# Final norm and stores inside the last group of the second feed-forward stage

## The chip, the cores and the metric

The kernel runs on one core of a Trainium2 chip. The metric is the time of one execution on the device in microseconds (us). The core has TensorE (PE: matmuls, and transposes through the matmul path), VectorE (DVE), ScalarE (ACT), GpSimd (POOL) and SyncE (SP, whose queue issues the DMAs). PSUM has eight banks of 128x512 f32.

## The reference

One decoder layer for 1024 prompt tokens and 64 sample tokens (8 sequences of 8), width 1024: a half-step feed-forward, a mixing block (RWKV and windowed attention), a second half-step feed-forward, and a final RMS norm. What the change touches is the end:

```python
x = x + 0.5 * gt3 * swiglu(modulate(x, norm_ffn2, sh3, sc3), ffn2_w_gu, ffn2_w_down)
y = x * lax.rsqrt(jnp.mean(x * x, axis=-1, keepdims=True) + 1e-5) * norm_final
```

The rows of y are stored as `y_prompt` (1024 x 1024) and `y_sample` (64 x 1024), f32.

## The kernel before

x lies transposed in SBUF: `k.x` is [128, 8, 1088], channel 128*c + p on partition p, chunk c, all 1088 tokens along the free axis. `ffn` (L657) is used for both feed-forward stages. It works in `NGRP` = 11 groups of 256 hidden channels. A group first makes the gate and up products, six pairs into PSUM banks 0 to 3 (`up`), with Silu on ACT (`swish`) and the product on DVE (`gated`), and then 24 down products (`down`): three token tiles t of 364, 364 and 360 tokens, and for each the eight output chunks c, so product v = 8*t + c, six matmuls in fp32r each (three passes over two hidden chunks). Product v goes into bank 4 + v % 4. `summed` on DVE adds it, gated, into x (`add_gated`, L490); for the third token tile, which has 296 prompt tokens and the 64 sample tokens, this is three instructions (L490, L493, L495), with a drain between the last two. The semaphore `dn_mm` says that a product is done, `dn_free` that its bank is free. In the second stage PE runs groups 1 to 10 in one loop. In the first stage (`first`) the last group is written out and has work of the next norm among its down products: square and mean (L338, L347), a root (L355) and scaling (L381).

After the second stage its block ends, and `store_output` (L2840) makes the final norm in a block of its own. It takes nine tiles of 128 tokens (the last has the 64 sample tokens), with two sets of buffers. For a tile DVE copies x into `x_now` (L2868), PE turns it in eight transposes into two banks (L2899), ACT squares both banks with row sums (L2911), DVE adds the two sums (L2875), ACT takes the root (L2915), DVE inverts it (L2877) and multiplies the two banks by it and by the norm's weight into `y_rows` (L2883), and SP stores the rows (L2930, L2932). The weight, one row broadcast over 128 partitions, is loaded at the start of that block (L2923). On each engine the tiles go in order; the loop body has two tiles.

Of the kernel before, what the change touches and what calls it, by code (L numbers as in the profile page):

```python
# [28 lines left out]
P = 128  # L29
D = 1024  # L30
# [625 lines left out]

def ffn(k, name, w_gu, w_down, i_shift):  # L657
# [35 lines left out]
    else:  # L693
        gate, gate_turned, gate_n = Ada(k, "gate2", [WT_AT + KB * a for a in (24, 32, 40, 48)], 7), k.psum[7][:, 256:512], 0
    LATE = range(1, 4) if first else range(1, 1)

    with nc.Block() as block:  # L697
        @block.sync
        def _(sp):
# [50 lines left out]
            if first:  # L750
                sp.wait_ge(up_lo_done, FC * NGRP)
                win.load(sp, 0, win.first[0])
                win.load(sp, 1, win.first[1])
                for t, (a, n) in enumerate(TILES):
                    sp.wait_ge(x_final, 2 * t + 2)
                    sp.dma_start(k.dram["x_spill"][:, :, a:a + n], k.x[:, :, a:a + n]).then_inc(k.spilled, 16)

        @block.gpsimd
        def _(pool):
# [22 lines left out]
            if first:  # L782
                win.low(pool, 0)
                mix.odd_lows(pool, 0)

        @block.tensor
        def _(pe):
# [8 lines left out]
            def down(g, t, c):  # L796
# [4 lines left out]
                pe.wait_ge(dn_free, ND * g + v + 1)  # L801
                three_passes(pe, k.psum[4 + v % 4][:, 0:n],
# [47 lines left out]
            def last_group():  # L850
# [6 lines left out]
                pe.wait_ge(dn_lo_done, g + 1)  # L857
                for t in range(NT):
# [16 lines left out]
            with pe.Fori(LATE.stop, NGRP - (1 if first else 0)) as g:  # L875
                group(g)
            if first:
                last_group()

        @block.scalar  # L880
        def _(act):
# [19 lines left out]
            if first:  # L901
# [5 lines left out]
                mix.highs(act, 0, True)  # L907

        @block.vector
        def _(dve):  # L910
# [25 lines left out]
            def summed(g, v):  # L936
                t, c = v // KD, v % KD
                dve.wait_ge(dn_mm, ND * g + v + 1)
                add_gated(dve, k, i_gate, c, t, k.psum[4 + v % 4], scratch[:, v % 2]).then_inc(dn_free, 1)
# [31 lines left out]
            def last_group():  # L971
# [3 lines left out]
                if not first:  # L975
                    for v in range(ND):
                        summed(g, v)
# [1862 lines left out]
def store_output(k):  # L2840

    x_now = [k.at(f"x_now{j}", WT_AT + 4096 * j, [P, KD, P]) for j in range(2)]
    rows = [k.at(f"y_rows{j}", WT_AT + 4096 * (2 + j), [P, D]) for j in range(2)]
    squares = k.at("y_squares", WT_AT + 4096 * 4, [P, D])
    weight = k.at("y_weight", WT_AT + 4096 * 5, [P, D])
    sums = [k.at(f"y_sums{j}", WT_AT + 4096 * 6 + 32 * j, [P, 4]) for j in range(2)]
    weight_in, now_done, turned, sq_done, sum_done, root_done, rows_done = (
        k.sem(f"y_{n}") for n in ("weight_in", "now_done", "turned", "sq_done", "sum_done", "root_done", "rows_done"))
    y_out = [k.sem(f"y_out{j}") for j in range(2)]
    NTT = NP_TOK // P  # L2850
    yv = k.dram["y_prompt"][0].rearrange("(i j p) n -> j p i n", p=P, j=2)

    def tiles(eng, body):

        with eng.Fori(0, NTT // 2 - 1) as i:  # L2855
            for j in range(2):
                body(i, j, P, P)
        body(NTT // 2 - 1, 0, P, P)
        body(NTT // 2 - 1, 1, P, NS_TOK)
        body(NTT // 2, 0, NS_TOK, 0)  # L2860

    with k.nc.Block() as block:  # L2862
        @block.vector
        def _(dve):
            def take(i, j, n):

                dve.wait_ge(turned, 2 * i + j + 1)
                dve.tensor_scalar(x_now[j][:, :, 0:n], k.x[:, :, bass.ds(256 * i + 128 * j, n)], 1.0, None, ALU.mult  # L2868
                                  ).then_inc(now_done, 1)

            def tile(i, j, n, n_next):
                if n_next:
                    take(i + j, 1 - j, n_next)
                dve.wait_ge(sq_done, 2 * i + j + 1)
                dve.tensor_tensor(sums[j][0:n, 2:3], sums[j][0:n, 0:1], sums[j][0:n, 1:2], ALU.add).then_inc(sum_done, 1)  # L2875
                dve.wait_ge(root_done, 2 * i + j + 1)
                dve.reciprocal(sums[j][0:n, 3:4], sums[j][0:n, 3:4])  # L2877
                dve.drain()  # L2878

                dve.wait_ge(y_out[j], 16 * i + 16)  # L2880
                for h in range(2):
                    col = slice(512 * h, 512 * h + 512)
                    ins = dve.scalar_tensor_tensor(rows[j][0:n, col], k.psum[2 * j + h][0:n, :], sums[j][0:n, 3:4],  # L2883
                                                   weight[0:n, col], ALU.mult, ALU.mult)
                ins.then_inc(rows_done, 1)

            dve.sem_inc(rows_done, 2)
            take(0, 0, P)
            dve.wait_ge(weight_in, 16)
            tiles(dve, tile)  # L2890

        @block.tensor
        def _(pe):
            def tile(i, j, n, n_next):
                pe.wait_ge(now_done, 2 * i + j + 1)

                pe.wait_ge(rows_done, 2 * i + j + 1)
                for c in range(KD):
                    ins = pe.transpose(k.psum[2 * j + c // 4][0:n, P * (c % 4):P * (c % 4) + P], x_now[j][:, c, 0:n],  # L2899
                                       k.c("ident"))  # L2900
# [77 lines left out]
```

## Time and profile before

| | us |
|---|---|
| median of 3 runs | 2534.65 |
| lowest, highest | 2529.38, 2535.4 |
| profiled execution | 2534.88 |
| its span | 2532.9 |
| PE busy in the span | 2401.2 (95%) |
| DVE busy | 1117.5 (44%) |
| ACT busy | 387.7 (15%) |
| POOL busy | 526.4 (21%) |

The profile is of one execution. Times in its rows count from the start of the span. A busy PE is not PE at its peak. PEclk is the clock granted to PE as a share of full speed: 1.00 is 2.4 GHz, 0.50 is 1.2 GHz. What an idle time is put down to is inferred from semaphores.

### The profile page before, as it was taken

What the parts mean: (1) busy time and instruction counts of PE and PEld (TensorE: products, weight loads), DVE (VectorE), ACT (ScalarE), POOL (GpSimd) and SP (SyncE); (2) the same over time, 40 slices, a digit from 0 to 9 for tenths busy, and PEclk for the clock granted to TensorE, in tenths of its full rate; (3) what the DMA queues carried; (4) which work ended last, traced back from release to release, by engine and by line L of the source; (5) the groups of instructions that cost most, each with busy time, mean ns of one, the idle gap of its engine ahead of it and who ended that gap; (6) DMA issues with size and microseconds to landing.
All of it is one profiled execution on the core that took longest, in us unless ns stands there. A gap on an engine that the chain in (4) does not pass through costs nothing. (4 is left out here: it accounts for less than half of the span.)

```text
span 2532.9 us, 51980 instructions
## 1 busy us (share of the span) xinstructions
PE 2401.2 (95%) x22210; PEld 2277.4 (90%) x22210; DVE 1117.5 (44%) x2477; ACT 387.7 (15%) x879; POOL 526.4 (21%) x270
## 2 busy tenths in 40 slices
PE   5999999999999899999788889989999999999996
PEld 4999999999999899888377775979999999999995
DVE  4533434333344454343666663137333444443336
ACT  4100000000000223344611132031000000000003
POOL 3312122121121131111511034123211212212200
PEclk8999999999999999999799997989999999999997
DMA  9223221111111221011310012122111111111102
GB/s 328 84 100 100 69 80 50 50 50 33 50 28 38 87 79 55 26 34 39 117 25 5 5 32 86 42 100 84 51 33 50 28 38 50 50 50 50 33 0 79
DMA packets 160616, 151.19 MB, mean 60 GB/s; under 512 B 21472, under 2 KB 141969, under 8 KB 160072
## 3 DMA queue, kind: packets, MB, share of 16 engines
q1 hardware_dynamic: 159944, 146.75, 18.3%
q8 instruction: 117, 1.92, 0.3%
q10 hardware_dynamic: 144, 2.23, 0.2%
q14 instruction: 27, 0.22, 0.0%
q0 software_dynamic: 384, 0.07, 0.0%
HBM read 137.98 MB, written 11.34 MB: 59 GB/s over the span
## 5 line engine op out<-in xcount | busy, mean ns | idle before, releaser
L475 PE MATMUL bank<-hh,f_up_hi 128*128 128x364 f32 (+1 forms) x2112 | 697.1, 330 | 9.4 <-ACT hh L415 9.4
L477 PE MATMUL bank<-hh,f_up_lo 128*128 128x364 f32 (+1 forms) x2112 | 695.1, 329 | 0.0
L476 PE MATMUL bank<-hl,f_up_hi 128*128 128x364 f32 (+1 forms) x2112 | 695.0, 329 | 0.0
L928 DVE TENSOR_TENSOR f_prod<-f_silu,bank 128x364 f32<-128x364 f32 x132 | 70.2, 532 | 779.7 <-PE bank L477 779.7
L475 PEld LDWEIGHTS bank<-hh,f_up_hi 128*128 128x128 f32 x2112 | 398.1, 188 | 15.8 <-issue 15.4
L490 DVE SCALAR_TENSOR_TENSOR x<-bank,mods,x 128x364 f32<-128x364 f32 (+2 forms) x552 | 310.4, 572 | 201.4 <-PE bank L477 184.4
L476 PEld LDWEIGHTS bank<-hl,f_up_hi 128*128 128x128 f32 x2112 | 398.2, 189 | 0.0
L477 PEld LDWEIGHTS bank<-hh,f_up_lo 128*128 128x128 f32 x2112 | 398.0, 188 | 0.0
L762 POOL TENSOR_TENSOR f_up_lo<-f_up_raw,f_up_hi 128x2048 fp32r<-128x2048 f32 x44 | 202.9, 4612 | 818.4 <-DVE f_up_hi L915 818.4
L475 PE MATMUL bank<-f_a_hi,f_dn_hi 128*128 128x364 f32 (+1 forms) x1056 | 347.4, 329 | 0.0
L477 PE MATMUL bank<-f_a_hi,f_dn_lo 128*128 128x364 f32 (+1 forms) x1056 | 346.9, 328 | 0.0
L476 PE MATMUL bank<-f_a_lo,f_dn_hi 128*128 128x364 f32 (+1 forms) x1056 | 346.9, 328 | 0.0
L887 ACT ACTIVATE f_silu<-bank 128x364 f32<-128x364 f32 x132 | 62.5, 474 | 1458.3 <-PE bank L477 1458.3
L475 PEld LDWEIGHTS bank<-f_a_hi,f_dn_hi 128*128 128x128 f32 x1056 | 198.5, 188 | 0.3
L476 PEld LDWEIGHTS bank<-f_a_lo,f_dn_hi 128*128 128x128 f32 x1056 | 198.5, 188 | 0.0
L477 PEld LDWEIGHTS bank<-f_a_hi,f_dn_lo 128*128 128x128 f32 x1056 | 198.5, 188 | 0.0
L767 POOL TENSOR_TENSOR f_dn_lo<-f_dn_raw,f_dn_hi 128x2048 fp32r<-128x2048 f32 x22 | 102.3, 4649 | 389.7 <-DVE f_dn_hi L921 389.7
L475 PE MATMUL bank<-hh,w_in_hi 128*128 128x364 f32 (+1 forms) x480 | 164.3, 342 | 9.1 <-PEq L697 8.2
L476 PE MATMUL bank<-hl,w_in_hi 128*128 128x364 f32 (+1 forms) x480 | 159.6, 333 | 0.0
L477 PE MATMUL bank<-hh,w_in_lo 128*128 128x364 f32 (+1 forms) x480 | 159.5, 332 | 0.0
L475 PEld LDWEIGHTS bank<-hh,w_in_hi 128*128 128x128 f32 x480 | 92.1, 192 | 22.2 <-issue 21.7
L1052 POOL TENSOR_TENSOR w_in_lo<-w_in_raw,w_in_hi 128x1024 fp32r<-128x1024 f32 x18 | 47.0, 2612 | 224.7 <-DVE w_in_hi L1047 224.7
(380 smaller groups left out, 2854.4 us busy)
## 6 DMA issues: line engine op xcount, KB each, us to landing
f_up_raw<-in_ffn_w_gu SPq DMA_DIRECT2D x88, 512.0 KB, 5.0
f_dn_raw<-in_ffn_w_down SPq DMA_DIRECT2D x22, 1024.0 KB, 7.6
ada<-in_w_ada SPq DMA_DIRECT2D x12, 1024.0 KB, 16.1
late<-in_w_ada SPq DMA_DIRECT2D x12, 1024.0 KB, 4.8
w_in_raw<-in_w_in SPq DMA_DIRECT2D x16, 512.0 KB
gates<-in_w_ada SPq DMA_DIRECT2D x8, 1024.0 KB, 7.0
x_in<-in_x_prompt SPq DMA_DIRECT2D x8, 512.0 KB, 8.8
gate<-in_w_ada SPq DMA_DIRECT2D x4, 1024.0 KB, 11.2
```

The source lines that it names most:

```text
L475: pe.matmul(out, wh, rh, start=(n == 0), stop=False)
L476: pe.matmul(out, wh, rl, start=False, stop=False)
L477: ins = pe.matmul(out, wl, rh, start=False, stop=(n == last))
L490: ins = dve.scalar_tensor_tensor(x[:, a:a + np_], bank[:, 0:np_], gate[:, 0:1], x[:, a:a + np_], ALU.mult, ALU.add)
L762: pool.tensor_tensor(up_lo[j][:], up_raw[:], up_hi[j][:].bitcast(F32), ALU.subtract).then_inc(up_lo_done, 1)
L767: pool.tensor_tensor(dn_lo[:], dn_raw[:], dn_hi[:].bitcast(F32), ALU.subtract).then_inc(dn_lo_done, 1)
L887: act.activation(silu[u % 2][:, 0:n], k.psum[2 * (u % 2)][:, 0:n], ACT.Silu).then_inc(gate_free, 1)
L928: dve.tensor_tensor(prod[u % 2][:, 0:n], silu[u % 2][:, 0:n], k.psum[2 * (u % 2) + 1][:, 0:n], ALU.mult).then_inc(up_free, 1)
L1052: pool.tensor_tensor(lo[:], self.raw_of(n)[:], hi[:].bitcast(F32), ALU.subtract).then_inc(self.lo_done, 1)
```

## The change

`store_output` goes. A class `Outputs` gives the same work to the block of the second feed-forward stage, where the last group is now written out.

- The nine tiles have 128, 128 and 108 tokens in each of the first two token tiles, and 128, 128 and 104 in the third (40 prompt and 64 sample tokens), so each lies in one token tile. They are turned straight from `k.x`, with no copy.
- A tile takes two banks: 0 and 1, 2 and 3, or 6 and 7. The down products of the third token tile use banks 4 and 5 alone. Each tile has its own row buffer (`y_rows0` to `y_rows8`), in the room of the weights that are used up.
- ACT takes an Identity of one sum (scaled, plus eps), then the Sqrt of the other with that as bias, in place of DVE's addition.
- Tiles 0 to 5 are handled whole between the products; of tiles 6 to 8 the first four chunks are turned after products 21 to 23 and squared, and DVE multiplies that half by the weight alone. After the last product chunks 4 to 6 and then 7 are turned, ACT squares the second half, DVE scales it, and POOL scales the first half by the inverse.
- The weight's load is issued when the last up weights have been split. Each tile has its store; the last has two.

```diff
+class Outputs:
+    TOKENS = [(0, 128), (128, 128), (256, 108), (364, 128), (492, 128), (620, 108), (728, 128), (856, 128), (984, 104)]
+    SETS = [0, 1, 0, 1, 0, 2, 1, 0, 2]
+    LAST = 6
...
+    def pe_tile(self, pe, j):
+        pe.wait_ge(self.x_final, j // 3 + 1)
+        if 2 <= j <= 4:
+            pe.wait_ge(self.rows_done, j - 1)
+        self.turn(pe, j, range(KD)).then_inc(self.turned, 1)
+
+    def pe_first_half(self, pe, j):
+        pe.wait_ge(self.x_final, 2 + 4)
+        pe.wait_ge(self.rows_done, j - 2)
+        self.turn(pe, j, range(4)).then_inc(self.turned, 1)
+
+    def pe_end(self, pe):
+        pe.wait_ge(self.x_final, 2 + KD - 1)
+        for j in range(self.LAST, len(self.TOKENS)):
+            self.turn(pe, j, range(4, KD - 1))
+        pe.wait_ge(self.x_final, 2 + KD)
+        for j in range(self.LAST, len(self.TOKENS)):
+            self.turn(pe, j, range(KD - 1, KD)).then_inc(self.turned, 1)
...
+    def root(self, act, j):
+        act.drain()
+        act.activation(self.col(j, 2), self.col(j, 1), ACT.Identity, scale=1.0 / D, bias=self.k.c("eps")[0:self.TOKENS[j][1]])
+        act.drain()
+        act.activation(self.col(j, 3), self.col(j, 0), ACT.Sqrt, scale=1.0 / D, bias=self.col(j, 2)).then_inc(self.root_done, 1)
+
+    def act(self, act):
+        for j in range(self.LAST):
+            act.wait_ge(self.turned, j + 1)
+            self.square(act, j, 0)
+            self.square(act, j, 1)
+            self.root(act, j)
+        for j in range(self.LAST, len(self.TOKENS)):
+            act.wait_ge(self.turned, j + 1)
+            act.drain()
+            self.square(act, j, 0).then_inc(self.squared, 1)
+        for j in range(self.LAST, len(self.TOKENS)):
+            act.wait_ge(self.turned, j + 4)
+            self.square(act, j, 1)
+            self.root(act, j)
...
+    def scaled(self, dve, j):
+        self.inverse(dve, j)
+        if j == 0:
+            dve.wait_ge(self.weight_in, 16)
+        for h in ((0, 1) if j < self.LAST else (1,)):
+            ins = dve.scalar_tensor_tensor(self.row(j, h), self.bank(j, h), self.col(j, 3),
+                                           self.weight[0:self.TOKENS[j][1], D // 2 * h:D // 2 * h + D // 2], ALU.mult, ALU.mult)
+        ins.then_inc(self.rows_done, 1)
...
 @@ sync
+            else:
+                sp.wait_ge(up_lo_done, FC * NGRP)
+                sp.dma_start(outputs.weight[:], k.dram["norm_final"].rearrange("(o n) -> o n", o=1).broadcast_to([P, D])
+                             ).then_inc(outputs.weight_in, 16)
+                outputs.sync(sp)
 @@ tensor, last group
+                    for c in range(KD):
+                        down(g, 0, c)
+                    pe.wait_ge(gate_free, NU * NGRP + 2)
+                    pe.wait_ge(up_free, NU * NGRP + 2)
+                    for c in range(KD):
+                        down(g, 1, c)
+                        if c in (1, 3, 5):
+                            outputs.pe_tile(pe, c // 2)
+                    for c in range(KD):
+                        down(g, 2, c, 2)
+                        if c in (0, 1, 2):
+                            outputs.pe_tile(pe, 3 + c)
+                        if c in (5, 6, 7):
+                            outputs.pe_first_half(pe, c + 1)
+                    outputs.pe_end(pe)
 @@ vector, last group
-                        summed(g, v)
+                        t, c = v // KD, v % KD
+                        summed(g, v, 2 if t == 2 else 4)
+                        if c == KD - 1 or t == 2:
+                            dve.drain().then_inc(outputs.x_final, 1)
+                        if t == 1 and c in (4, 6):
+                            outputs.scaled(dve, c // 2 - 2)
+                        if t == 2 and c in (0, 2, 3, 5):
+                            outputs.scaled(dve, (2, None, 3, 4, None, 5)[c])
+                        if t == 2 and c >= 6:
+                            outputs.weighted(dve, c)
+                    outputs.weighted(dve, 8)
+                    for j in range(outputs.LAST, len(outputs.TOKENS)):
+                        outputs.scaled(dve, j)
 @@ build
-        store_output(k)
```

## Rows read from the trace of the kernel before

**Rows 1.** Windows: busy us of PE, PEld, DVE, ACT, POOL; PEclk, DMA share, GB/s.

```profile
2480.00:2490.00 10.00, 10.00 (x62) 10.00 (x61) 6.86 (x17) 0.00 (x0) 0.00 (x0) 1.00 0.00 0
2500.00:2534.00 34.00, 15.69 (x64) 12.22 (x64) 19.23 (x44) 17.91 (x45) 0.00 (x0) 0.50 0.34 131
```

**Rows 2.** Timeline, last products and sums: start, duration, what, idle before.

```profile
2482.97 0.60 DVE L490 SCALAR_TENSOR_TENSOR x<-bank,mods,x 128x364 f32<-128x364 f32 x1 [0.41 <-PE bank L477]
...
2493.58 0.33 PE L477 MATMUL bank<-f_a_hi,f_dn_lo 128*128 128x360 f32 x1
...
2493.95 0.53 DVE L490 SCALAR_TENSOR_TENSOR x<-bank,mods,x 128x296 f32<-128x296 f32 x1
...
2494.70 0.23 DVE L495 TENSOR_TENSOR x<-x,f_scratch 128x64 f32<-128x64 f32 x1
```

**Rows 3.** Timeline of PE, transposes of the first two tiles.

```profile
2496.10 1.10 PE L2899 MATMUL bank<-const,x_now 128*128 128x128 f32 x8 [2.19 <-DVE x_now L2868]
2500.07 1.97 PE L2899 MATMUL bank<-const,x_now 128*128 128x128 f32 x8 [2.87 <-DVE x_now L2868]
```

**Rows 4.** The chain that ended last: start, us, what.

```profile
2495.17 3.80 DMA y_weight<-in_norm_final
```

**Rows 5.** Timeline of DVE in the store stage, a tile and the last rows.

```profile
2503.89 0.16 DVE L2877 RECIPROCAL y_sums<-y_sums 128x1 f32<-128x1 f32 x1 [0.36 <-ACT y_sums L2915]
2504.13 1.41 DVE L2883 SCALAR_TENSOR_TENSOR y_rows<-bank,y_sums,y_weight 128x512 f32<-128x512 f32 x2
2505.46 0.68 DVE L2868 TENSOR_SCALAR x_now<-x 128x1024 f32 x1
...
2528.18 1.40 DVE L2883 SCALAR_TENSOR_TENSOR y_rows<-bank,y_sums,y_weight 64x512 f32<-64x512 f32 x2
```

**Rows 6.** ACT: timeline of one tile, then its table loads by line.

```profile
2502.07 0.60 ACT L2911 ACTIVATE y_squares<-bank 128x512 f32<-128x512 f32 x1 [1.67 <-PE bank L2899]
...
2503.14 0.20 ACT L2911 ACTIVATION_READ_ACCUMULATOR y_squares<-bank 128x1 f32 x1
2503.57 0.29 ACT L2915 ACTIVATE y_sums<-y_sums,const 128x1 f32<-128x1 f32 x1 [0.23 <-DVE y_sums L2875]
...
L2911 ACT ACT_TABLE_LOAD x3 | 3.8, 1283 | 29.8 <-PEq L697 28.9 <-issue 1.0
L2915 ACT ACT_TABLE_LOAD x3 | 3.8, 1283 | 0.1
```

**Rows 7.** Timeline in the first stage's last group, where norm work lies among products.

```profile
854.31 1.28 ACT L355 ACT_TABLE_LOAD   x1
856.06 1.46 PE L347 MATMUL bank<-mix_sq,const 128*32 128x91 f32 x64
858.75 0.60 DVE L490 SCALAR_TENSOR_TENSOR x<-bank,mods,x 128x364 f32<-128x364 f32 x1 [1.99 <-PE bank L477]
869.14 0.23 DVE L495 TENSOR_TENSOR x<-x,f_scratch 128x64 f32<-128x64 f32 x1
869.48 0.59 DVE L381 SCALAR_TENSOR_TENSOR mix_t<-x,mods,bank 128x364 f32<-128x364 f32 x1
```

**Rows 8.** Windows with a pausing PE, from the mixing block; columns as in rows 1.

```profile
1250.00:1255.00 5.00, 1.75 (x24) 0.81 (x28) 4.83 (x13) 3.69 (x10) 4.72 (x7) 0.75 0.37 141
...
1400.00:1405.00 5.00, 2.79 (x162) 2.39 (x150) 3.85 (x8) 0.31 (x1) 1.95 (x4) 1.00 0.01 3
```

**Rows 9.** POOL by line: op, shapes, count, busy us, mean ns, idle before.

```profile
L2083 POOL TENSOR_TENSOR decays<-const,p_end 128x512 f32<-128x512 f32 x4 | 4.3, 1099 | 0.0
...
L1223 POOL COPY q_new<-qkv 128x256 f32<-128x256 f32 x1 | 0.4, 395 | 0.0
```

**Rows 10.** Stores: the last issue (timeline of SP), and a window during a 128-row store.

```profile
2529.61 0.55 SPq L2932 DMA_DIRECT2D out_y_sample<-y_rows  x1
...
2503.80:2504.20 0.40, 0.40 (x4) 0.40 (x3) 0.23 (x2) 0.06 (x1) 0.00 (x0) 0.50 1.03 420
```

More of the change, by code:

```diff
@@ L784, in _ @@
                 mix.odd_lows(pool, 0)
+            else:
+                outputs.pool(pool)
         @block.tensor
@@ L794, in up, with down @@
                                    k.hl[:, c, a:a + n]) for c in range(KD)]).then_inc(done, 1)
-            def down(g, t, c):
+            def down(g, t, c, banks=4):
                 a, n = TILES[t]
@@ L874, in _ @@
                     group(g, True)
-            with pe.Fori(LATE.stop, NGRP - (1 if first else 0)) as g:
+            with pe.Fori(LATE.stop, NGRP - 1) as g:
                 group(g)
-            if first:
-                last_group()
+            last_group()
         @block.scalar
@@ L2837, in _ @@
                         add_gated(dve, k, 5, 2 * i + j, t, k.psum[3 * j + t], scratch[:, j]).then_inc(bank_free, 1)
[L2840 to L2900, printed above, removed]
-                ins.then_inc(turned, 1)
-            pe.sem_inc(turned, 2)
-            tiles(pe, tile)
-        @block.scalar
-        def _(act):
-            def tile(i, j, n, n_next):
-                act.wait_ge(turned, 2 * i + j + 3)
-                for h in range(2):
-                    ins = act.activation(squares[0:n, 512 * h:512 * h + 512], k.psum[2 * j + h][0:n, :], ACT.Square,
-                                         accum_out=sums[j][0:n, h:h + 1])
-                ins.then_inc(sq_done, 1)
-                act.wait_ge(sum_done, 2 * i + j + 1)
-                act.activation(sums[j][0:n, 3:4], sums[j][0:n, 2:3], ACT.Sqrt, scale=1.0 / D, bias=k.c("eps")[0:n]
-                               ).then_inc(root_done, 1)
-                act.drain()
-            tiles(act, tile)
-        @block.sync
-        def _(sp):
-            sp.dma_start(weight[:], k.dram["norm_final"].rearrange("(o n) -> o n", o=1).broadcast_to([P, D])
-                         ).then_inc(weight_in, 16)
-            for j in range(2):
-                sp.sem_inc(y_out[j], 16)
-            with sp.Fori(0, NTT // 2) as i:
-                for j in range(2):
-                    sp.wait_ge(rows_done, 2 * i + j + 3)
-                    sp.dma_start(yv[j][:, bass.ds(i, 1)].rearrange("p o n -> p (o n)"), rows[j][:]).then_inc(y_out[j], 16)
-            sp.wait_ge(rows_done, NTT + 3)
-            sp.dma_start(k.dram["y_sample"].rearrange("s t n -> (s t) n"), rows[0][0:NS_TOK, :]).then_inc(y_out[0], 16)
-            sp.wait_ge(y_out[0], 16 * (NTT // 2 + 2))
-            sp.wait_ge(y_out[1], 16 * (NTT // 2 + 1))
-            sp.wait_ge(k.cache_out, 16 * 3)
```

59 lines of the change are left out of this document (55 added, 4 removed).

## The prediction

> **What bounds the kernel now.** I read the windows by stage first, then the timelines of the last products and of the store stage, then the chain. While the last group runs, TensorE (PE) is busy in every microsecond at the full clock, and VectorE (DVE) is busy 6.86 of 10 us; in the 34 us after 2500 PE is busy 15.7 us at clock 0.50, so that stretch is bound by something else [rows 1]. The last matmul starts at 2493.58, and the last sum into x ends at 2494.93 (2494.70 + 0.23) [rows 2]. The last row of y is ready at 2529.58 (2528.18 + 1.40) [rows 5]. These 34.65 us hold only the final norm of nine tiles. They are a round trip per tile (copy, eight transposes, squares, sum, root, inverse, two products), opened by a load of the norm's weight that nothing covers, 3.80 us [rows 4], with ScalarE's (ACT) tables changed six times at 1.28 us [rows 6] and the transposes of a tile at 1.97 us, where the first tile took 1.10 at the full clock [rows 3]. From the last row to the end of the span another 3.32 us pass.
>
> **What the change moves.** The work per tile goes among the products of the last group: tiles 0 to 2 are turned on PE after products 9, 11 and 13 (I number the 24 down products 0 to 23, eight per token tile of 364), tiles 3 to 5 after 16, 17 and 18, first halves of 6 to 8 after 21, 22 and 23, and the rest behind 23. DVE scales tiles 0 to 5 after products 12, 14, 16, 18, 19 and 21. SyncE (SP) and GpSimd (POOL) have nothing else left: their queues wait for rows, and nobody stands behind them. The weight is now asked for as soon as the last up weights are split, before the group's products, and lands well ahead of its use. The nine copies into x_now, the added barrier and most table loads are gone.
>
> **Prices.** A down product: 1.00 us on PE (the starts of 2482.97 and its neighbours, idle 0.41 + busy 0.60), and DVE starts 0.2 us after PE could go on [rows 2]. A sum of the first two token tiles holds DVE 0.51 us (0.60, the next may start 0.09 before its end, as 2504.13 + 1.41 against 2505.46 shows [rows 5]). A sum of the third has three instructions and gives 0.98 us [rows 2]; with the new drain the next starts 0.11 after its end (869.14 + 0.23 to 869.48) instead of 0.09 before, so 1.09 us [rows 7]. Scaling a tile: reciprocal to product 0.24, then 1.32 to the next instruction, 1.56 in all, rows ready after 1.65 [rows 5]. The half rows of tiles 6 to 8: 0.66 on DVE by half of the same row. Turning a tile: eight transposes at the full clock, pitch 0.12, 0.95 us [rows 3]; in the first feed-forward stage 64 small matmuls in 1.46 us put between two products moved DVE's next start by 1.59 (idle 1.99 for 0.40), so changing over costs up to 0.2 [rows 7]: 1.15 per tile. Bounds 0.95 and 1.97. A root on ACT: two squares with their sums 1.27 (2502.07 to 2503.34), then an Identity and a Sqrt of 0.29 each and two drains, 2.0 us in all [rows 6]; for tile 0 one table load of 1.28, since the straight code of the first stage has a single one, at its root [rows 7]. POOL's product of 128x512 is not in the trace: a copy of half its size took 0.395, a two-input product of its size 1.10; I take 0.8, as there is one tensor input [rows 9].
>
> **The sum, along the engine that ends last.** DVE starts the sum of product 12 at 2482.97 + 0.02 + two tiles turned before it at 1.15 = 2485.3. It scales tile 0 (turned at 2481.1; ACT needs 2.0 and the load of 1.28 and has the root at 2484.4, 1.4 us before DVE asks, so the load is covered) and is free at 2487.4. Behind that wait stands the sum of product 13, done by PE at 2486.1, and PE itself waits from 2486.1 to 2487.5, because tile 2 needs the banks of tile 0: 1.4 us lost. Tile 2 and product 14 take 1.15 + 1.0 + 0.2: DVE at 2489.9. Sum 14, tile 1, sum 15 with drain, sum 16, tile 2, sum 17: 0.51 + 1.56 + 0.71 + 1.09 + 1.56 + 1.09 gives 2496.4. PE waits for rows of tile 2 at 2495.4, turns tile 4 and makes product 18: DVE goes on at 2497.8. From there DVE never rests: sums 18 to 22 (5 x 1.09) and tiles 3, 4 and 5 (3 x 1.56) give 2507.9, the half rows of tile 6 0.66, and sum 23 with its drain 1.07: x is final at 2509.65. That is 14.7 us later than in the kernel before. PE's own work from product 8 on, 16 x 1.0 + 6 x 1.15 + 3 x 0.58 = 24.6 us after 2477.8, would end at 2502.4, so in the third token tile DVE is the bound, and with two banks instead of four PE is held to its pace. Then the end: PE turns the last chunk of tile 6 and ACT begins, 0.38 us: 2510.0. ACT needs 1.47 per tile (one square with its sum 0.78, two small instructions, drains) and gives the third root at 2514.45; DVE's two small half rows and POOL lie beside it. Reciprocal 0.16, hand-over 0.1 and POOL 0.8 give 2515.5 (DVE's own half is ready at 2515.4). The stores: 3.32 us as before, and 0.6 more, because the last tile has two DMAs, one behind the other, and an issue takes 0.55 [rows 10]. Span 2519.4, against 2532.9: 13.5 us less. The profiled execution took 2534.88 us for a span of 2532.9, 1.98 outside it; the median of the runs is 2534.65, so both are the same kernel to 0.01%. The forecast is 2519.4 + 2.0 = 2521.4 us.
>
> **What could be off by little.** Turning at 0.95: 0.8 us less. No price for the drains: 1.4 less; drains at 0.35: 1.0 more. The last transposes at half clock: 0.8 more. POOL at 0.4 or 1.1: 0 or 0.3 more. Stores of the last three tiles overlap: a 128-row store moves 420 GB/s, so 512 KB need about 1.3 us, and rows come each 1.47 us; a queue of up to 0.5 us is possible [rows 10]. Together this gives savings of 11.5 to 15.5 us, so 2519.4 to 2523.4.
>
> **Rivals.**
> *The clock falls while PE waits (slower than before at its far end).* Place: from product 8 on PE is cut by tiles and waits. Price: each product then takes 2.0 and each tile 1.9 to 2.0 (1.97 against 1.10 [rows 3]); PE becomes the bound again. Done as above with these prices, a fall at product 14 leaves a saving of 2.4 us (2532.5), a fall at product 18 one of 7.7 us (2527.2), and a fall at product 8 that lasts to the end costs 4.6 us, 2539.5. The sign turns at about product 11. For it: PE is at work some 17 of the 22 us between 2484.7 and 2507, with waits of 1.4 us; with 1.75 of 5 us busy the clock was 0.75 elsewhere. Against it: with 2.79 of 5 us busy, in pieces, it stayed at 1.00 [rows 8], and the transposes of the first tile, 1.10 us, ran at the full clock after 2 us of rest [rows 3]. The Trainium skill speaks against this change here: "TensorE: Matmul & The Clock Gate", section "A second HAM failure mode: psum-queue depth-cycling", says that a PE that pauses often between groups of matmuls, because it cycles through PSUM banks, falls to the lower clock again and again; by that rule the time is the 2532.5 of this rival. The two rows named before it disagree with each other on how much pausing is enough, and no row shows exactly this pattern.
> *The tables are changed at every tile.* Place: ACT, squares and root of each tile. In the loop of the store stage each of three passes has a load at the Sqrt and one at the Square [rows 6]. Price: 2.57 more for each root; ACT then sets the pace of the scaling and of the end, and the saving shrinks to 1.1: 2533.8. Against it: the straight code of the first stage has one load for two squares and a root [rows 7]. The Trainium skill, "ScalarE: Activation LUTs", section "Table sets: the hidden batching unit", says to batch by set and prices a switch at about 2.66 us, load and drain; an estimate from that page, two switches at each of nine roots, would be 24 us slower than before, 2558. Here the loads at the Sqrt take 1.28 us with 0.1 us idle before all three of them [rows 6], so the trace does not show that drain.
> *DVE pays more for its small steps* (waits, reciprocals, drains at 0.3 to 0.5 us more for each of the six tiles and eight sums of the last third): a saving of 8 to 11.5, 2523.4 to 2527.
> *It does not do what it says*: were the tiles held until the last sum, nothing of this would hold; but the waits in the diff count sums up to each tile's own, so I give it nothing.
>
> **How the numbers follow.** Forecast 0.68; DVE dearer 0.10; clock falling from product 14 or later 0.13; clock low from the start 0.04; tables at every tile 0.05. The range that leaves no more than 2 in 10 out takes in the forecast, the dearer steps and the mildest clock case: 2517 to 2527; it goes below 2519.4 because the three runs of before spread from 2529.38 to 2535.4. A measurement of this kernel tells about 0.3%, 7.6 us, from no change: faster means under 2527.0. That is 0.68 + 0.10 and a quarter of the clock case: 0.81. The rest of that case, the tables and part of the low clock are within 0.3%: 0.16. Slower by more: 0.03, since even the low clock from product 8 costs only 4.6 us and needs another cost beside it.
>
> **What would show it.** The last sum into x ends at about 2509.6, and in the last 15 us before it DVE has no idle time while PE waits for DVE: right. PE waits near tile 2 for rows of tile 0, 1.4 us. PEclk 1.00 between 2480 and 2508; any 0.5 there means the first rival. One table load of 1.28 in the whole stretch; more mean the second. Three roots 1.5 us apart at the end, then 1 us to the last rows and 3.9 to the end of the span. If PE, not DVE, is busy throughout the third token tile, my price of the scaling was too high or the clock too low.

## The result and the profile after

The changed kernel takes 2514.43 us (median of 4 runs, 2513.45 to 2516.04), beside 2532.02 us for the kernel before (median of 4, 2527.93 to 2535.4): a ratio of 0.9932, 95% interval 0.9913 to 0.9951. The profiled execution took 2516.04 us, its span is 2514.2 us. The direction was right; the size was not: 17.6 us less instead of 13.5, and 2.6 us below the lower bound of 2517.

The spans of the two profiles differ by 18.7 us (2532.9 and 2514.2). To see in which part the error lies I measure both traces from one event that the change doesn't touch: the start of DVE's sum of product 2 in the last group (2472.99 before, ten products ahead of the row of product 12 in [rows 2]; 2467.61 after). I call the stretch from there to the end of the span **the tail**. It is 59.91 us before and 46.59 us after: 13.3 us less, where 13.5 was forecast. The other 5.4 us lie ahead of every instruction of the norm.

The windows of the kernel after (busy us of PE, PEld, DVE, ACT, POOL; PEclk, DMA share, GB/s) answer [rows 1]:

```profile
2480.00:2490.00 10.00, 7.00 (x47) 6.11 (x46) 7.57 (x18) 4.29 (x14) 0.00 (x0) 1.00 0.26 105
2490.00:2500.00 10.00, 8.49 (x57) 7.83 (x55) 7.54 (x22) 4.92 (x16) 0.00 (x0) 1.00 0.40 151
2500.00:2504.00 4.00, 2.65 (x18) 1.66 (x16) 3.59 (x10) 1.01 (x4) 0.00 (x0) 1.00 0.32 111
2504.00:2514.20 10.20, 0.00 (x0) 0.00 (x0) 3.42 (x8) 3.33 (x12) 4.66 (x3) 0.60 0.38 145
```

PE is no longer busy all the time, but its clock stays at 1.00 until its last transpose. The stretch without any matmul is now 10 us instead of the 34 with few of them.

DVE's timeline after (start, us, what, idle before), from the sum of product 2 on, then around the first scaled tile and the last idle time:

```profile
2467.61 0.60 DVE L490 SCALAR_TENSOR_TENSOR x<-bank,mods,x 128x364 f32<-128x364 f32 x1 [0.34 <-PE bank L477]
...
2479.34 0.60 DVE L490 SCALAR_TENSOR_TENSOR x<-bank,mods,x 128x364 f32<-128x364 f32 x1 [1.27 <-PE bank L477]
2479.85 0.15 DVE L734 RECIPROCAL y_sums<-y_sums 128x1 f32<-128x1 f32 x1
2480.10 1.41 DVE L743 SCALAR_TENSOR_TENSOR y_rows<-bank,y_sums,y_weight 128x512 f32<-128x512 f32 x2
2481.42 0.59 DVE L490 SCALAR_TENSOR_TENSOR x<-bank,mods,x 128x364 f32<-128x364 f32 x1
2483.74 0.60 DVE L490 SCALAR_TENSOR_TENSOR x<-bank,mods,x 128x364 f32<-128x364 f32 x1 [1.73 <-PE bank L477]
...
2491.54 0.53 DVE L490 SCALAR_TENSOR_TENSOR x<-bank,mods,x 128x296 f32<-128x296 f32 x1 [1.36 <-PE bank L477]
...
2503.05 0.23 DVE L495 TENSOR_TENSOR x<-x,f_scratch 128x64 f32<-128x64 f32 x1
```

After 2491.54 (product 18's sum) DVE has no idle time until x is final at 2503.28. PE waits for it at the tiles; its timeline:

```profile
2474.41 1.04 PE L686 MATMUL bank<-const,x 128*128 128x128 f32 x8
...
2481.65 1.06 PE L686 MATMUL bank<-const,x 128*108 128x128 f32 x8 [1.36 <-DVE y_rows L743]
2486.51 1.09 PE L686 MATMUL bank<-const,x 128*128 128x128 f32 x8 [0.80 <-DVEq L1121]
2489.44 1.06 PE L686 MATMUL bank<-const,x 128*128 128x128 f32 x8 [0.84 <-DVE y_rows L743]
```

The end of the kernel after, in the timelines of ACT, POOL and SP (the table load from further up):

```profile
2477.18 1.28 ACT L715 ACT_TABLE_LOAD   x1
...
2503.73 0.60 ACT L709 ACTIVATE y_squares<-bank 128x512 f32<-128x512 f32 x1 [1.48 <-PE bank L686]
...
2504.85 0.30 ACT L715 ACTIVATE y_sums<-y_sums 128x1 f32<-128x1 f32 x1
...
2505.53 4.66 POOL L756 TENSOR_SCALAR y_rows<-y_rows,y_sums 128x512 f32<-128x512 f32 x3 [81.98 <-DVE y_sums L734]
...
2506.15 0.29 ACT L715 ACTIVATE y_sums<-y_sums 128x1 f32<-128x1 f32 x1
...
2507.45 0.29 ACT L715 ACTIVATE y_sums<-y_sums 104x1 f32<-104x1 f32 x1
...
2510.63 0.60 SPq L767 DMA_DIRECT2D out_y_sample<-y_rows  x1
```

There is one table load in this stretch. The three roots come 1.30 us apart. POOL needs 4.66 us for three half tiles, 1.55 each, and with 2510.19 is the last to finish; 4.01 us later the span ends.

### The profile page after: what moved, and what is told of

Same layout as the page of the kernel before. It is cut to its first block and busy times, and to the rows that moved or that the text cites. A ratio compares the mean times of both kernels' runs of the same rounds, so it can differ in the third digit from the quotient of the medians.

```text
span 2514.2 us, 51860 instructions
## 1 busy us (share of the span) xinstructions
PE 2387.4 (95%) x22210; PEld 2268.4 (90%) x22210; DVE 1109.5 (44%) x2459; ACT 383.7 (15%) x883; POOL 531.2 (21%) x273
```

## The experiments

Two questions were open: where the 5.4 us ahead of the change came from, and which part of the change brings the 13.3 us. Tails are read from one profiled execution of each kernel. They may be compared: the stretch of the second feed-forward stage from its first Silu to the sum of product 2 lasts 757.1 us in all of them. How much a tail varies by itself is known from two pairs only: 46.59 and 46.54 for the changed kernel, 59.91 and 59.36 for the one before. Where lines of code shifted, the line numbers in the rows differ a little.

### The same kernels again (a1_before, a2_after)

No edit: `a1_before` is the kernel before, `a2_after` the changed one.

> The kernel before, unchanged, once more. Two theories of the 5.4 us by which the two profiled executions differ ahead of the last group (product 2 is summed at 2472.99 in the one and at 2467.61 in the other). Theory 1, chance: the mixing block lasts up to some 6 us longer in some executions of any kernel, because the clock falls at another moment in it; then the executions of this kernel lie in 2527 to 2536 again, on both sides of 2532, and the stretch from the sum of product 2 to the end of the span is 59.9 us within 0.3 in the profile, wherever that sum lies. Theory 2, the change shortened the mixing block: then the unchanged kernel shows the late sum (2472 to 2474) in its profile and has few executions under 2530.

> The changed kernel once more. Theory 1, chance: some of its executions are 4 to 7 us longer than the shortest, so some lie at 2518 to 2522, and the median of many is about 13.3 us under that of the kernel before. Theory 2, the change itself: all executions stay within 3 us of 2514.5, and the saving is 17 to 19 us against the kernel before. Both: from the sum of product 2 to the end 46.6 us within 0.3.

Measured: 2530.22 us for the kernel before (12 runs, 2525.82 to 2537.1; ratio to its other runs 0.9997, 0.9986 to 1.0008), 2515.46 for the changed one (5 runs, 2514.71 to 2518.09; ratio 0.9943, 0.993 to 0.9956). The tails are 59.36 (0.55 us off the 59.9 that was expected within 0.3) and 46.54. The event that starts the tail lies at 2468.54 in `a1_before`, 4.45 us earlier than in the first profile of the same kernel, and only 0.9 us after that of the changed one. So 4.5 of the 5.4 us between the profiles also appear between two executions of one and the same kernel. The times of the changed kernel decide less: of its five runs the longest, 2518.09, just reaches the 2518 to 2522 of the first theory, and the saving between the medians is 14.8 us, between the 13.3 of the first and the 17 to 19 of the second.

Where they arise: from the last Silu of the first feed-forward stage to the first Silu of the second, the mixing block, it takes 875.69 us in the first profile of before, 871.90 in `a1_before`, 870.14 in the profile after. The window from 1500 to 1600 us, in which nothing differs between the programs, in the profile before, in `a1_before` and after:

```profile
1500.00:1600.00 100.00, 97.13 (x961) 66.77 (x960) 38.28 (x63) 25.26 (x46) 39.95 (x34) 0.85 0.28 84
```

```profile
1500.00:1600.00 100.00, 96.92 (x988) 68.50 (x985) 39.05 (x66) 26.73 (x48) 41.93 (x35) 0.90 0.28 84
```

```profile
1500.00:1600.00 100.00, 97.12 (x989) 69.03 (x989) 39.06 (x66) 26.09 (x47) 42.12 (x34) 0.90 0.28 84
```

The granted clock is 0.85 in the first and 0.90 in the other two, although the first two are the same program. The kernels further down repeat this: with 0.85 or 0.86 in this window the mixing block took 874.6 to 878.7 us (three of them and the first profile of before), with 0.88 to 0.91 (all the others) it took 869.2 to 872.0. More than half of the 3.8 us between the two executions of the kernel before arise in one place inside the window. In the profile before, then in `a1_before`:

```profile
1532.00:1536.00 4.00, 4.00 (x10) 0.99 (x10) 0.61 (x1) 1.15 (x2) 2.75 (x2) 0.52 0.01 2
```

```profile
1532.00:1536.00 4.00, 4.00 (x44) 2.10 (x43) 0.98 (x2) 1.60 (x2) 2.91 (x2) 1.00 0.01 2
```

PE is shown busy throughout both. The same four matmuls in PE's timeline, before and in `a1_before`:

```profile
1532.75 1.97 PE L2272 MATMUL bank<-k_seq,vk_tok 64*64 64x512 f32 x4
```

```profile
1531.86 1.08 PE L2272 MATMUL bank<-k_seq,vk_tok 64*64 64x512 f32 x4
```

Between 1530 and 1538 us the first execution falls 2.4 us behind the second. Why the clock stays low longer at this place in some executions is open.

### All of the norm behind the products (e3_norm_behind, e9_behind_4_sets)

`e3_norm_behind` keeps the changed tile (turned straight from x, ACT's Identity in place of DVE's sum, one table load, a row buffer and an early weight) but does all nine tiles whole after product 23 (no halves, nothing on POOL), with three sets of banks as in the changed kernel; `e9_behind_4_sets` gives them four.

```diff
 @@ e3_norm_behind, against the kernel after
-    LAST = 6
+    LAST = 9
+    BEFORE = [0, 0, 1, 2, 3, 0, 4, 5, 6]
...
-                        if c in (1, 3, 5):
-                            outputs.pe_tile(pe, c // 2)
...
-                        down(g, 2, c, 2)
...
+                        down(g, 2, c)
+                    for j in range(9):
+                        outputs.pe_tile(pe, j)
 @@ e9_behind_4_sets, against e3_norm_behind
-    SETS = [0, 1, 0, 1, 0, 2, 1, 0, 2]
+    SETS = [0, 1, 2, 3, 0, 1, 2, 3, 0]
-    BEFORE = [0, 0, 1, 2, 3, 0, 4, 5, 6]
+    BEFORE = [0, 0, 0, 0, 1, 2, 3, 4, 5]
```

> The changed kernel with all of the norm's work behind product 23: the same block, the same instructions per tile, straight code, row buffers and early weight, but nothing among the products, and four banks for all products. It tells what the overlap with the products is worth apart from the leaner tile. Theory L, lean: most of the saving comes from the leaner tile (one table load, no copy, no sum on DVE, three sets of banks), ACT sets the pace at 1.97 us per tile; from product 2's sum to the end 24 us of products, then 0.3 + 1.1 + 1.28 + 9 x 1.97 + 1.7 + 3.8, together 47.5 to 49 us, where the kernel before has 59.9 and the changed one 46.6. Theory O, overlap: the tiles are the cost, at 3.4 us each as in the store stage of the kernel before, and only hiding them among products pays; then the stretch is 55 us or more.

Measured: 2523.06 us (8 runs, 2520.7 to 2526.85; ratio 0.9974, 0.9963 to 0.9984), a tail of 51.61. That is above the one theory's band and far below the other's. ACT's timeline names the difference, two waits for PE:

```profile
2499.45 0.60 ACT L710 ACTIVATE y_squares<-bank 108x512 f32<-108x512 f32 x1 [1.94 <-PE bank L687]
...
2505.26 0.60 ACT L710 ACTIVATE y_squares<-bank 128x512 f32<-128x512 f32 x1 [1.93 <-PE bank L687]
```

Tiles 2 and 4 need the banks of tiles 0 and 2, and PE, at half clock, starts on them only when DVE has scaled those. With four sets both waits should go:

> The kernel with the norm behind product 23 (e3_norm_behind) and four sets of two banks in place of three. There ACT worked at 1.89 us per tile but waited twice 1.94 us for PE, since tiles 2 and 4 need the banks of tiles 0 and 2. If these two waits are what separates it from its forecast, the stretch from product 2's sum to the end goes from 51.6 to 47.7 us, and hiding the norm among the products is worth 1.1 us alone against the changed kernel's 46.6. If PE at half the clock, 2.0 us a tile, takes their place, it is 49 us or more and the overlap is worth 2.5 or more.

Measured: 2517.01 us (4 runs, 2510.04 to 2518.12; ratio 0.993, 0.9909 to 0.9951), a tail of 47.52 where 47.7 was expected. ACT runs without a rest, 1.88 us for a tile (the roots of tiles 1 and 2):

```profile
2497.11 0.29 ACT L716 ACTIVATE y_sums<-y_sums 128x1 f32<-128x1 f32 x1
...
2498.99 0.29 ACT L716 ACTIVATE y_sums<-y_sums 108x1 f32<-108x1 f32 x1
```

This is the finding on the change itself: 11.8 to 12.4 of its 13 us can be had with no work among the products, by a tile that costs less and enough banks. Putting two thirds of the work among the products brings only 0.9 us more (47.52 against 46.59). That holds beside the version with four sets, which it can have because no products need banks any more; beside `e3_norm_behind`, with the three sets of the changed kernel and with PE at half clock at its waits, the overlap brings 5.0 us (51.61 against 46.59). How much of the leaner tile is the table loads, the copy or the sum was not tried one by one. Why the overlap brings so little is seen at the last sum into x, in DVE's timeline of `e9_behind_4_sets`:

```profile
2490.80 0.23 DVE L495 TENSOR_TENSOR x<-x,f_scratch 128x64 f32<-128x64 f32 x1
```

Here x is final 22.65 us after the start of the tail (2468.38), in the changed kernel 35.67 us after it.

### The weight's load alone (e4_weight_early)

The kernel before, with the norm's weight loaded ahead of the last group's down products.

```diff
+            else:
+                sp.wait_ge(up_lo_done, FC * NGRP)
+                sp.dma_start(k.y_weight[:], k.dram["norm_final"]...).then_inc(k.y_weight_in, 16)
...
-            sp.dma_start(weight[:], k.dram["norm_final"]...).then_inc(weight_in, 16)
```

> The kernel before, with one part of the change alone: the norm's weight is loaded as soon as the last up weights are split, in the second stage's block. The chain of waits gives that load 3.80 us; DVE waits 3.27 us for it. If the chain is right, the stretch from product 2's sum to the end shrinks by 3.3 to 3.8 us, to 56.1 to 56.6. If ACT's tables decide (its Sqrt load ends at 2499.8 and its first root at 2500.4 whatever the weight does), only ACT's idle 1.67 us ahead of the second tile's squares goes: 58.2.

Measured: 2528.16 us (11 runs, 2524.38 to 2537.31; ratio 0.9996, 0.9985 to 1.0006), a tail of 58.94, which is 0.4 us below `a1_before` and 1.0 below the first profile. That is far above the 56.1 to 56.6 of the chain and 0.7 above the 58.2 of the other theory, and hardly more than the 0.55 us by which the two profiles of the kernel before differ. The load of 3.80 us opened the chain [rows 4], yet it is worth less than a third of itself. ACT's timeline, first in `e4_weight_early`, then in `a1_before`: table load and root of the first tile, first square of the second:

```profile
2493.89 1.28 ACT L2920 ACT_TABLE_LOAD   x1
2495.18 0.29 ACT L2920 ACTIVATE y_sums<-y_sums,const 128x1 f32<-128x1 f32 x1
2495.93 0.60 ACT L2916 ACTIVATE y_squares<-bank 128x512 f32<-128x512 f32 x1 [0.45 <-issue]
```

```profile
2494.06 1.28 ACT L2915 ACT_TABLE_LOAD   x1
2495.36 0.30 ACT L2915 ACTIVATE y_sums<-y_sums,const 128x1 f32<-128x1 f32 x1
2497.09 0.60 ACT L2911 ACTIVATE y_squares<-bank 128x512 f32<-128x512 f32 x1 [1.44 <-PE bank L2899]
```

The first tile's root has nothing to do with the weight and comes at 2495.2 to 2495.4 in both. Only the second tile's squares gain: 1.16 us in these rows, 0.98 from the start of each tail (2468.36 and 2468.54), and a part of that is lost again behind.

### Is DVE the bound in the third token tile? (e5_few_drains)

The drains after the sums of the third token tile are kept only where somebody asks for a final x; PE's waits count those that are left.

```diff
-                        if c == KD - 1 or t == 2:
+                        if c == KD - 1 or t == 2 and c in (3, 6):
                             dve.drain().then_inc(outputs.x_final, 1)
```

> The changed kernel without five of the eight drains behind the sums of the third token tile (kept behind its chunks 3, 6 and 7, which are the ones PE waits for). If DVE is the bound there, as the prediction has it, each drain gone is 0.20 us: the stretch from the sum of product 2 to the end of the span goes from 46.6 to 45.6 us. If PE or the banks set the pace, it stays at 46.4 to 46.7.

Measured (one execution): a tail of 45.73, 0.8 to 0.9 us less, where 45.6 was expected if DVE is the bound. A sum now gives way to the next after 0.14 us (2498.86 to 2499.00) instead of 0.34 for the same pair after (2497.61 to 2497.95):

```profile
2498.86 0.23 DVE L495 TENSOR_TENSOR x<-x,f_scratch 128x64 f32<-128x64 f32 x1
2499.00 0.52 DVE L490 SCALAR_TENSOR_TENSOR x<-bank,mods,x 128x296 f32<-128x296 f32 x1
```

### Is POOL on the path at the end? (e6_act_half, e7_both)

The first half of the last tile is scaled by ACT, so that POOL has two halves instead of three; `e7_both` has this and the fewer drains.

```diff
+        j = len(self.TOKENS) - 1
+        act.wait_ge(self.half_done, 3)
+        act.wait_ge(self.inv_done, j + 1)
+        act.activation(self.row(j, 0), self.row(j, 0), ACT.Identity, scale=self.col(j, 3)).then_inc(self.half_by_act, 1)
...
-        for n, j in enumerate(range(self.LAST, len(self.TOKENS))):
+        for n, j in enumerate(range(self.LAST, len(self.TOKENS) - 1)):
```

> The changed kernel with the first half of the last tile scaled on ACT in place of POOL. POOL's products took 1.55 us each (the prediction had 0.8) and end 1.4 us behind DVE's. If POOL ends the chain, the stretch from product 2's sum to the end shrinks by 1.1 to 1.4 us, to 45.2 to 45.5. If the stores behind it decide (512 KB of tile 7 still under way), it shrinks by less than 0.5.

Measured (one execution): a tail of 46.07, 0.5 us less instead of the 1.1 to 1.4 that would follow if POOL alone ended the chain. POOL, DVE and ACT now end within 0.14 us of each other:

```profile
2506.24 3.11 POOL L760 TENSOR_SCALAR y_rows<-y_rows,y_sums 128x512 f32<-128x512 f32 x2 [81.97 <-DVE y_sums L738]
...
2508.74 0.75 DVE L747 SCALAR_TENSOR_TENSOR y_rows<-bank,y_sums,y_weight 104x512 f32<-104x512 f32 x1
2508.75 0.72 ACT L734 ACTIVATE y_rows<-y_rows,y_sums 104x512 f32<-104x512 f32 x1 [0.29 <-DVE y_sums L738]
...
2510.22 0.60 SPq L773 DMA_DIRECT2D out_y_sample<-y_rows  x1
```

From the last row (2509.49) to the end it is now 4.9 us, against 4.01 from the last row after. Counted from the start of the tail the last row comes 1.4 us earlier, and 0.9 of that turned into a longer wait for stores.

> The two edits together: drains only where a final x is asked for, and the last tile's first half scaled on ScalarE instead of GpSimd. Stretch from VectorE's sum of product 2 to the end of the span; each alone gave 45.73 and 46.07 against 46.59 and 46.54. If the gains add: 45.2. If the stores behind the last rows set the end, the two together give no more than either alone: 45.5 to 45.8.

Measured (one execution): a tail of 45.30, 1.3 us less than after: the two gains (0.8 and 0.5) add up. The run itself took 2522.98 us, because this execution has a clock of 0.85 in the window above and 878.7 us of mixing block: a single time says nothing about an edit of 1 us here.

### What sets the last 5 us (e10_two_queues, e12_half_stores)

`e10_two_queues` is `e7_both` with the sample's store on ACT's queue, beside SP's. `e12_half_stores` stores tiles 6 and 7 by halves as well, each half when it is ready, and swaps the last tile's two stores.

```diff
 @@ e10_two_queues (act, after its last half)
+        act.wait_ge(self.half_by_act, 1)
+        act.wait_ge(self.rows_done, j + 1)
+        act.dma_start(self.k.dram["y_sample"]..., self.rows[j][NP_TOK - a:n, :]).then_inc(self.y_out, 16)
 @@ e12_half_stores (sync)
+            if self.LAST <= j < len(self.TOKENS) - 1:
+                sp.dma_start(k.dram["y_prompt"][0, a:a + n, D // 2:D], self.row(j, 1)).then_inc(self.y_out, 16)
+                sp.wait_ge(self.half_scaled, j - self.LAST + 1)
+                sp.dma_start(k.dram["y_prompt"][0, a:a + n, 0:D // 2], self.row(j, 0)).then_inc(self.y_out, 16)
+                continue
```

> As e7_both, and the store of the sample's rows is issued by ScalarE's queue beside SyncE's store of the prompt's rows, instead of 0.6 us behind it. If the issue of the last store is on the path: a stretch of 44.6 to 44.8. If the bytes of the tiles before are still on their way and set the end: 45.2, nothing gained. The median of the runs against the kernel before, by 14 to 15 us for the changed kernel and 2 us less here: a ratio of 0.9935 within 0.001 either way, since the clock in the mixing block moves single runs by more than the 2 us.

Measured: 2518.02 us (6 runs, 2514.19 to 2518.8; ratio 0.9939, 0.9923 to 0.9955), a tail of 45.30, the same as `e7_both`. So the last issue was not on the path. What is left are the bytes. The windows from the last row to the end, first of `e10_two_queues`, then of `e12_half_stores`:

```profile
2510.40:2515.40 5.00, 0.00 (x0) 0.00 (x0) 0.06 (x1) 0.03 (x1) 0.00 (x0) 0.50 0.64 234
```

```profile
2515.40:2519.80 4.40, 0.00 (x0) 0.00 (x0) 0.07 (x1) 0.04 (x1) 0.00 (x0) 0.50 0.61 211
```

At 234 GB/s for 5.0 us some 1170 KB are still to go when the last row is ready. The DMA engines are not busy to the very end: in the last microsecond of `e10_two_queues` their share is 0.03. The expectation below is wrong in this point.

> As e10_two_queues, but the rows of tiles 6 and 7 are stored by halves: VectorE's half as soon as it is ready, the other when GpSimd has scaled it; the last tile's prompt rows go from ScalarE's queue, its sample rows from SyncE's. In e7_both and e10_two_queues the span ends 4.95 us after the last row with all DMA engines busy until then at up to 413 GB/s: the first of the three last stores goes out only when GpSimd is done with tile 6. If bytes queued behind the last rows set the end: about 672 KB instead of 940 KB are left when the last row is ready, the stretch from VectorE's sum of product 2 falls from 45.3 to 44.2 to 44.6. If the end is set by what follows the last issue (its latency of some 3.3 to 3.6 us): the last issue comes no earlier than before, two more issues stand ahead of it, and the stretch is 45.3 or more.

Measured: a tail of 44.66, 0.64 us less and 0.06 above the band that goes with the bytes; in the 4.4 us after the last row 930 KB go instead of 1170 (both more than I had reckoned, since the store of tile 6 was also under way). So fewer bytes queued behind the last rows bring the end nearer, and the last row is 4.3 us ahead of it. Whether bytes still set the end here isn't shown: the last issue (2515.80 + 0.60) ends 3.4 us ahead of it, where it was 2.7 us in the kernel before [rows 10]. It is the shortest tail of the versions that compute everything, 1.9 us below the change. The median of its 6 runs is 2517.46 us (2510.63 to 2521.84; ratio 0.9941, 0.9926 to 0.9956), which can't be told from the changed kernel's: the mixing block moves single runs by more.

### Rows on ACT and POOL (e8_act_pool_rows, e11_pool_one_input)

To relieve DVE, `e8_act_pool_rows` (on top of `e7_both`) lets ACT scale tiles 2 and 4 and POOL multiply them by the weight. `e11_pool_one_input` changes POOL's instruction to a product with one column; it leaves out the norm's weight for these two tiles.

```diff
 @@ e8_act_pool_rows
+            if j in self.BY_ACT:
+                act.wait_ge(self.inv_done, j + 1)
+                for h in range(2):
+                    ins = act.activation(self.row(j, h), self.bank(j, h), ACT.Identity, scale=self.col(j, 3))
+                ins.then_inc(self.act_scaled, 1)
...
+            pool.tensor_tensor(self.rows[j][0:n, :], self.rows[j][0:n, :], self.weight[0:n, :], ALU.mult).then_inc(self.pool_rows, 1)
 @@ e11_pool_one_input, against e8_act_pool_rows
-            pool.tensor_tensor(self.rows[j][0:n, :], self.rows[j][0:n, :], self.weight[0:n, :], ALU.mult).then_inc(self.pool_rows, 1)
+            pool.tensor_scalar(self.rows[j][0:n, :], self.rows[j][0:n, :], self.col(j, 3), None, ALU.mult).then_inc(self.pool_rows, 1)
```

> A version meant to be faster: few drains and ACT's half as in the two others, and the rows of tiles 2 and 4 scaled on ACT (two Identities with the inverse as scale) and multiplied by the weight on POOL, which takes 2 x 1.32 us off DVE in the third token tile. If DVE is the bound there, the stretch from product 2's sum to the end is 46.6 - 1.0 - 1.3 - 2.6 = 41.7 us, and the whole 2510 to 2511 us where the changed kernel has 2515.4. If PE takes over as the bound earlier, or POOL's two-input product of 128x1024 (2.4 us) slows DVE's, 43 to 45 us.

Measured: 2516.4 us (6 runs, 2514.32 to 2522.48; ratio 0.9942, 0.9926 to 0.9958), a tail of 45.96: 4.3 us above what was hoped for, and worse than `e7_both` without the edit. POOL's and DVE's timelines:

```profile
2488.25 2.38 POOL L772 TENSOR_TENSOR y_rows<-y_rows,y_weight 108x1024 f32<-108x1024 f32 x1 [65.47 <-ACT y_rows L732]
2494.62 2.39 POOL L772 TENSOR_TENSOR y_rows<-y_rows,y_weight 128x1024 f32<-128x1024 f32 x1 [3.99 <-ACT y_rows L732]
...
2488.61 2.10 DVE L495 TENSOR_TENSOR x<-x,f_scratch 128x64 f32<-128x64 f32 x1
...
2495.18 1.92 DVE L495 TENSOR_TENSOR x<-x,f_scratch 128x64 f32<-128x64 f32 x1
```

The addition of 64 columns, 0.23 us everywhere else, took 2.10 and 1.92: both times it started while POOL was at its product and ended 0.1 us after POOL. Together they took 3.6 us longer than elsewhere.

> The kernel e8_act_pool_rows with one instruction changed: GpSimd's product of tiles 2 and 4 with the weight (two tensors from SBUF, 128x1024) becomes a product of the same rows with one column (one tensor, the norm's weight is left out for these two tiles). If it is GpSimd's second tensor that holds up VectorE: the sums into x that start during GpSimd's instruction take 0.23 us as elsewhere, not 2.10 and 1.92, and the stretch falls from 45.96 to 42 to 43. If any large GpSimd instruction does it: about 1.9 us again, or longer, as the instruction takes some 3.1 (2 x 1.55), and the stretch stays at 46 or above.

Measured (one execution): a tail of 44.41, between the two theories (42 to 43, and 46 or above).

```profile
2488.56 2.85 POOL L772 TENSOR_SCALAR y_rows<-y_rows,y_sums 108x1024 f32<-108x1024 f32 x1 [65.52 <-ACT y_rows L732]
2494.61 2.85 POOL L772 TENSOR_SCALAR y_rows<-y_rows,y_sums 128x1024 f32<-128x1024 f32 x1 [3.20 <-ACT y_rows L732]
...
2488.87 0.88 DVE L495 TENSOR_TENSOR x<-x,f_scratch 128x64 f32<-128x64 f32 x1
...
2495.15 0.65 DVE L495 TENSOR_TENSOR x<-x,f_scratch 128x64 f32<-128x64 f32 x1
...
2496.46 0.23 DVE L495 TENSOR_TENSOR x<-x,f_scratch 128x64 f32<-128x64 f32 x1
```

POOL's instruction is longer now and holds DVE up less. Both additions end 1.19 us after POOL's start (2489.75, 2495.80), and a third one (2496.46), in the middle of POOL's instruction, is not held up at all. So it is not true that only a second tensor on POOL disturbs DVE, nor that any large POOL instruction does so for its whole length: with two tensors DVE's addition was held to POOL's end, with one for the first 1.2 us. What POOL does in those 1.2 us is open. DVE's additions gained 1.22 and 1.27 us, the tail 1.55; the rest went into a wait of 0.85 us for PE at 2490.60.

## Why the prediction was right in its mechanism and wrong in its number

**The failed step: what stands for the kernel before.** The prediction says of the profiled execution and the median of three that "both are the same kernel to 0.01%" and subtracts the tail's gain from that one execution. They agreed with each other by chance: the 62 runs of that kernel on record besides `a1_before` have a median of 2531.05 us (2526.38 to 2541.46). The third of the three runs shown, 5 us below the other two, had already told of it. From `a1_before`, with the tail's gain as forecast, the number is 2530.2 - 13.5 = 2516.7; from the shared 2532.02 of the result's own runs it is 2518.5. The measured 2515.46 and 2514.43 are still 1 and 4 us lower. Differences of this size arise in the mixing block, which takes 869.2 to 878.7 us in single executions and is longer where the clock is lower; that this is the whole of the remainder is not shown. Whether the clock falls less often in the changed kernel or all 9 of its runs (2513.45 to 2518.09) were spared by chance is open too. For chance speaks that versions with the same mixing block were not spared (`e7_both`, `e10_two_queues`, `e12_half_stores`), and that the median less the tail follows no edit: 2467.8 and 2468.9 us for the changed kernel, 2472.1 and 2470.9 for the one before, 2472.7 and 2472.8 for `e10_two_queues` and `e12_half_stores`, which differ from the changed kernel only behind that point. The lower bound of 2517 allowed 2.4 us for this where single executions differ by 5 and more.

**The tail, term by term.** Forecast 46.4 us (2519.4 less 2472.99), measured 46.59. The terms:

- *Products, sums and tiles up to the final x*: forecast 36.66 us after the start of the tail, measured 35.67 (2503.28). Of the 0.99 us, 0.56 lie in the first two tiles turned: product and tile together take 1.87 us (sums at 2474.61 and 2476.48), so a tile costs 0.87 and not 1.15. It was even below the lower bound of 0.95, which had been taken from transposes behind an idle PE.
- *Waits of PE*: 1.4 us forecast at tile 2, 1.36 measured. The waits of 0.80 and 0.84 at tiles 3 and 4 are there as well; the prediction names the second, without a size.
- *DVE as the bound*: forecast from the sum of product 18 on 11.85 us without a rest, measured 11.74 (2491.54 to 2503.28); `e5_few_drains` shows it by experiment. The scaling of a tile is 1.57 to 1.59 (1.56), a sum with its drain 1.08 to 1.09 (1.09).
- *The roots at the end*: pitch 1.30 instead of 1.47; together with the first one the third root comes 4.46 us after x is final instead of 4.80.
- *POOL's product*: 1.55 us instead of 0.8, and above the upper bound of 1.1. This term was mis-sized: it had been placed between a copy of half the size and a product with two inputs [rows 9], and a product with a column is slower than either. As POOL has three in a row, the last rows are ready 2.45 us after the third root instead of 1.05.
- *The stores*: 3.92 forecast, 4.01 measured. That they agree is half luck: 0.6 for the second issue was not what counted. As soon as rows come earlier (`e6_act_half`) most of the gain is lost to the stores.

In sum -0.99 - 0.34 + 1.40 + 0.09 = +0.16. Two errors of 1 us and more cancelled, so the agreement of the total is better than the steps deserve.

**Where the gain comes from** was told wrongly. The prediction speaks of work that "goes among the products". `e9_behind_4_sets` gets all but 0.9 us of it with all work behind them. In the changed kernel DVE, which has the sums, became the bound in the third token tile, and x became final 13 us later. And the 3.80 us of weight load that "nothing covers" were worth 0.4 to 1.0 us (`e4_weight_early`): the table load and root of the first tile lie beside it and stay where they were.

**The rivals.** The clock did not fall: 1.00 in all windows up to 2504, although PE was busy only 7.00 of 10 us around its longest waits. So the rule of the Trainium skill ("TensorE: Matmul & The Clock Gate", section "A second HAM failure mode: psum-queue depth-cycling"), by which the time would have been 2532.5, does not agree with this trace, in which PE waits 0.8 to 1.4 us at a time. The tables were loaded once, at 1.28 us, in straight code. DVE's small steps cost what had been taken.

## What to carry to other kernels

Compare two kernels from an event that both have, not by the span, when a stretch ahead of the change varies from run to run, and take the spread of such stretches into the range. Before a step is put under another engine's work, ask what it costs done lean and behind it, with enough buffers: here that alone was 12 of 13 us, and the overlap, which made the last x final 13 us later, added 0.9. With fewer buffers the overlap is worth more (5.0 us beside three sets of banks). At the end of a kernel count the bytes still to be stored when the last row is ready, and send what is ready in smaller pieces.

## What was not expected of the hardware

- An addition on DVE of two SBUF tensors, 128x64, took 2.10 and 1.92 us instead of 0.23 beside a POOL product of two SBUF tensors, 128x1024, of 2.4 us, and ended with it; DVE instructions with an input from PSUM, started just behind POOL's, kept their 0.21 us (at 2488.31 and 2494.87). The Trainium skill says that the two engines share their SBUF interfaces and contend when DVE's instruction has two SBUF inputs ("GPSIMD Engine Reference", section "1. Specifications"); the trace agrees, and adds the size. Beside a POOL product with a column the same addition was held only until 1.19 us after POOL's start.
- POOL's in-place product of 128x512 with a column took 1.55 us, longer for each element than its two-input product of 128x1024 (2.39).
- The same mixing block has a granted clock of 0.85 to 0.86 or of 0.88 to 0.91 in the same 100 us of different executions, also of one and the same program, and takes 874.6 to 878.7 or 869.2 to 872.0 us for that block.
